# Half of the output projection's contraction as three fp32r products, with the first expert weights split ahead of the expert stage

## The reference

```python
qkv = modulate(x) @ w_in                          # 640 x 1024 @ 1024 x 3072
na_o = neighbourhood_or_dense_attention(...)      # 8 heads x 64
df_o = rms_norm(softmax(q1 k1) v - lam * softmax(q2 k2) v) * (1 - lambda_init)   # 4 heads x 128
o = concat([na_o, df_o])                          # 640 x 1024
x1 = layer_norm(ALPHA * x + gate1 * (o @ w_out))  # w_out 1024 x 1024
aff = softmax(modulate(x1) @ w_router)            # 16 experts
g, idx = top_k(aff.T, cap)                        # 64 latent + 16 context tokens for each expert
y = (silu(xs @ w_gate) * (xs @ w_up)) @ w_down * g       # d_ff 2816, fp32 weights, 553 MB in all
out = layer_norm(ALPHA * x1 + gate2 * scatter_add(y))
```

## Time and profile before

| | us |
|---|---|
| median of 3 runs (lowest, highest) | 2013.46 (2012.74, 2016.18) |
| the profiled execution | 2015.8 |
| its span, first to last instruction | 2014.0 |
| PE busy | 1940.7 (96%) |
| DVE busy | 1651.3 (82%) |
| ACT busy | 1378.8 (68%) |
| POOL busy | 182.9 (9%) |

### The profile page before, as it was taken

The page is one execution under the profiler, slowest core; times in us unless marked ns, Lnnn a source line. Parts: engine busy times, 40 slices in busy tenths (PEclk is TensorE's granted clock), DMA queues, the critical chain, the costliest instruction groups (busy, mean ns, idle before and its releaser), DMA issues.

```text
span 2014.0 us, 25015 instructions
## 1 busy us (share of the span) xinstructions
PE 1940.7 (96%) x9564; PEld 1327.3 (66%) x9564; DVE 1651.3 (82%) x1627; ACT 1378.8 (68%) x1618; POOL 182.9 (9%) x98
## 2 busy tenths in 40 slices
PE   8999889984999999999999999999999999999998
PEld 8999666652666666666666666666666666666664
DVE  3766556677989889898989898988989898989896
ACT  3222255644787877778787878787777878787875
POOL 0000212121010101010101101010101010110100
PEclk9999789995999999999999999999999999999999
DMA  9544601133999999999999999999999999999994
GB/s 380 198 155 170 218 27 54 58 117 125 405 343 407 362 413 359 388 376 372 385 369 394 360 398 348 404 355 401 360 384 376 374 387 368 393 360 395 353 388 158
DMA packets 100998, 636.32 MB, mean 316 GB/s; under 512 B 11569, under 2 KB 19761, under 8 KB 28049
## 3 DMA queue, kind: packets, MB, share of 16 engines
q1 hardware_dynamic: 96048, 618.23, 78.5%
q0 software_dynamic: 4832, 16.50, 3.2%
HBM read 620.02 MB, written 13.88 MB: 315 GB/s over the span
## 4 chain that ended last, share of the span: by engine, by line
PE 75%; ACT 1%; DVE 1%; issue 0%; DVEq 0%; ACTq 0%
PE ps L1430 16%; PE ps L1429 16%; PE ps L1434 16%; PE ps L1446 8%; PE ps L1447 8%; PE ps L1451 8%; PE ps L1409 1%; PE ps L1400 0%; DVE place L1608 0%; ACT place L1533 0%; DVE place L1550 0%; PE ps L1469 0%; ACT place L1497 0%; ACT place L1536 0%; ACT L1536 0%; ACT place L1531 0%
## 5 line engine op out<-in xcount | busy, mean ns | idle before, releaser
L1550 DVE TENSOR_TENSOR place<-ring,place 128x2048 fp32r<-128x2048 f32 x528 | 1226.6, 2335 | 150.8 <-ACT place L1497 147.4
L1497 ACT ACTIVATE place<-ring 128x2048 fp32r<-128x2048 f32 x528 | 1010.1, 1916 | 334.1 <-PE ps L1434 234.3
L1429 PE MATMUL ps<-place 128*80 128x512 f32 x1408 | 561.0, 398 | 4.9 <-DVE place L1544 4.9
L1430 PE MATMUL ps<-place 128*80 128x512 f32 x1408 | 555.5, 395 | 0.0
L1434 PE MATMUL ps<-place 128*80 128x512 f32 x1408 | 381.4, 392 | 0.0
L1434 PEld LDWEIGHTS ps<-place 128*80 128x80 f32 x1408 | 208.2, 148 | 115.8 <-issue 0.7
L1429 PEld LDWEIGHTS ps<-place 128*80 128x80 f32 x1408 | 208.5, 148 | 110.5 <-DVE place L1544 5.1
L1446 PE MATMUL ps<-place 128*80 128x512 f32 x704 | 280.5, 398 | 0.0
L1430 PEld LDWEIGHTS ps<-place 128*80 128x80 f32 x1408 | 209.2, 149 | 107.2 <-issue 0.7
L1447 PE MATMUL ps<-place 128*80 128x512 f32 x704 | 277.1, 394 | 0.0
L1451 PE MATMUL ps<-place 128*80 128x512 f32 x704 | 190.4, 392 | 0.0
(11 more groups left out here) (189 smaller groups left out, 1708.4 us busy)
## 6 DMA issues: line engine op xcount, KB each, us to landing
ring<-in_w_exp SPq DMA_DIRECT2D x528, 1024.0 KB, 7.1
ring<-in_w_late SPq DMA_DIRECT2D x16, 1024.0 KB, 11.0
ring<-in_w_in SPq DMA_DIRECT2D x12, 1024.0 KB, 6.9
ring<-in_w_ada SPq DMA_DIRECT2D x8, 1024.0 KB, 10.2
ring<-in_w_out SPq DMA_DIRECT2D x4, 1024.0 KB, 6.3
place<-in_near_bias SPq DMA_DIRECT2D x16, 256.0 KB, 3.2
ring<-in_xT SPq DMA_DIRECT2D x4, 640.0 KB, 9.1
place<-in_x SPq DMA_DIRECT2D x5, 512.0 KB, 6.5
```

The source lines that it names most:

```text
L1429: eng.matmul(out, xH[:, e % 2, kk, :], w, start=(kk == 0), stop=False)
L1430: eng.matmul(out, xL[:, e % 2, kk, :], w, start=False, stop=False)
L1497: eng.activation(wH[:, n % SPLITS, :], ring[:, slot("exp", n), :], ACT.Copy).then_inc(wh_done, 1)
L1550: eng.tensor_tensor(wL[:, n % SPLITS, :], ring[:, slot("exp", n), :], wH[:, n % SPLITS, :].bitcast(F32), ALU.subtract).then_inc(chunk_used, 1)
```

## The change

1. **Output projection.** For contraction tiles 0 to 3 of each half the product is three fp32r products. ACT rounds `out` chunks 0 and 2 into two free ring slots in steps 1 and 2 (`round_out`), POOL writes the remainders over the raw chunks (two tensor_tensor of 128 x 2048). ACT copies the first half of the turned tile into `OTH` (rounded); DVE takes the remainder `OTL` from PSUM (`split_turned`, first thing in the step after "turn o"). Tiles 4 to 7 stay fp32. PE waits for the new semaphores `out_split` and `ot_split`.
2. **Ring.** The two free slots are those that the first two expert chunks had. All four `out` chunks are issued in the first block, no expert chunk is; the six first expert chunks are issued when the last tile's projection has let their slots go, three after half 0 and three after half 1.
3. **First expert chunks.** `high(0)`, `high(1)` run at the end of ACT's attention block, `low(0)`, `low(1)` on POOL, after its last `start_sum` and ahead of the gather.
4. **Projection block.** The rotary products come after `values(i, 0)`, the context keys' transposes after `values(i, 2)`.
5. **Memory.** Tiles are packed anew (`mod_c` in `scr`, `tie` and `rowA` in `far`, `Xg` and others moved).

```diff
-                for n in range(n, FIRST + 2):
+                for n in range(n, FIRST):
                     issue(eng, n)
...
-                for n in range(FIRST + 2, FIRST + RING):
+                eng.wait_ge(out_used, 2)
+                for n in (FIRST + 3, FIRST + 2, FIRST):
+                    issue(eng, n)
+                eng.wait_ge(out_used, 4)
+                for n in (FIRST + 5, FIRST + 4, FIRST + 1):
                     issue(eng, n)
...
+        def out_high(half):
+            return ring_rounded[:, (FIRST + half) % RING, :]
+        def out_low(half):
+            return ring_rounded[:, slot("out", 2 * half), :]
...
                 for k in range(STEPS):
+                    if k in (1, 2):
+                        eng.wait_ge(out_rounded, k)
+                        eng.tensor_tensor(out_low(k - 1), ring[:, slot("out", 2 * (k - 1)), :], out_high(k - 1).bitcast(F32),
+                                          ALU.subtract).then_inc(out_split, 1)
...
                     start_sum(s)
+                for n in range(READY):
+                    low(eng, n)
...
+                        if j < HALF_K:
+                            eng.matmul(ps[:, bank, :], OTH[:, j, :], wh, start=(j == 0), stop=False)
+                            eng.matmul(ps[:, bank, :], OTL[:, j, :], wh, start=False, stop=False)
+                            mm = eng.matmul(ps[:, bank, :], OTH[:, j, :], wl, start=False, stop=(j == final))
...
+                def round_out(half):
+                    arrived(eng, "out", 2 * half)
+                    eng.wait_ge(*released(FIRST + half - RING))
+                    eng.activation(out_high(half), ring[:, slot("out", 2 * half), :], ACT.Copy).then_inc(out_rounded, 1)
...
+                def split_turned(s, part, tiles):
+                    use = turn_no["o", s, part]
+                    eng.wait_ge(t_copied, use + 1)
+                    c0 = P * (part == 2)
+                    n = P * len(tiles)
+                    out, high = (x[:, tiles[0]:tiles[-1] + 1, :].rearrange("p k t -> p (k t)") for x in (OTL, OTH))
+                    eng.tensor_tensor(out, ps[:, 4 + use % 2, c0:c0 + n], high.bitcast(F32), ALU.subtract).then_inc(ot_split, 1)
...
                 for k in range(STEPS):
+                    if due("turn o", k - 1) is not None:
+                        split_turned(due("turn o", k - 1), 0, range(HALF_K))
                     if 1 <= k:
                         combine(k - 1)
```

More of the change, by code:

```diff
@@ L82, in sem @@
             return ctx.enter_context(nc.semaphore(name))
+        with nc.sbuf_tensor("ring_rounded", [P, RING, CW], F32R) as ring_rounded:
+            pass
         ring = ctx.enter_context(nc.sbuf_tensor("ring", [P, RING, CW], F32))
@@ L119, in build @@
         places.append(ctx.enter_context(ExitStack()))
-        qna, qdf = (b.rearrange("p (i t) -> p i t", i=GROUPS) for b in (shared, take(GROUPS * TOK)))
-        Xg = shared[:, 0:2 * D].rearrange("p (b d) -> p b d", b=2)
-        X32 = shared[:, 2 * D:2 * D + HALF_K * CAP].rearrange("p (k s) -> p k s", k=HALF_K)
+        qna, qdf = (take(GROUPS * TOK).rearrange("p (i t) -> p i t", i=GROUPS) for _ in range(2))
         kna, kdf = (take(GROUPS * (TOK + CTX)).rearrange("p (i t) -> p i t", i=GROUPS) for _ in range(2))
@@ L323, in _ @@
                         project(i, g)
-                    for t in range(3):
-                        values(i, t)
+                    values(i, 0)
                     if i == 0:
@@ L338, in _ @@
                     mm.then_inc(kctx_ready, 1)
+                    values(i, 3)
                     values(i, 4)
@@ L402, in _ @@
                         high(3 * i + 3)
-                    for t in range(4):
+                    for t in range(3):
                         copy_values(i, t)
@@ L635, in build, with splits_by, high, low @@
             turn_no[use] = len(turn_no)
+        def splits_by(n):
+            return sum(1 for use, m in turn_no.items() if m <= n and use[0] == "o" and use[2] in (0, 2))
         def turned(s):
-            return OT if s < END else Pb[:, UNITS % 2, 0:D].rearrange("p (k t) -> p k t", k=KT)
+            return OT if s < END else Pb[:, UNITS % 2, 0:D // 2].rearrange("p (k t) -> p k t", k=HALF_K)
+        def out_high(half):
+            return ring_rounded[:, (FIRST + half) % RING, :]
+        def out_low(half):
+            return ring_rounded[:, slot("out", 2 * half), :]
         def heads_of(s, part):
             return range(GROUPS) if s < END else (range(3), range(3, GROUPS))[part]
+        def high(eng, n):
+            arrived(eng, "exp", n)
+            eng.activation(wH[:, n % SPLITS, :], ring[:, slot("exp", n), :], ACT.Copy).then_inc(wh_done, 1)
+        def low(eng, n):
+            eng.wait_ge(wh_done, n + 1)
+            eng.tensor_tensor(wL[:, n % SPLITS, :], ring[:, slot("exp", n), :], wH[:, n % SPLITS, :].bitcast(F32),
+                              ALU.subtract).then_inc(chunk_used, 1)
         def fetch(eng, e):
@@ L1028, in _ @@
                     eng.wait_ge(t_ready, use + 1)
-                    eng.activation(turned(END)[:, HALF_K * part:HALF_K * part + 3, :].rearrange("p k t -> p (k t)"),
+                    eng.activation((turned(END) if part else OTH)[:, 0:3, :].rearrange("p k t -> p (k t)"),
                                    ps[:, 4 + use % 2, 0:3 * P], ACT.Copy).then_inc(t_copied, 1)
@@ L1040, in _ @@
                 raise_logits(END)
+                for n in range(READY):
+                    high(eng, n)
             @block.vector
@@ L1245, in _ @@
                 share(END - 2)
+                split_turned(END, 0, range(3))
                 gated(END - 1, 1)
@@ L1250, in _ @@
                 keep_shares(END - 2)
+                split_turned(END, 2, range(3, 4))
                 first_half(range(0, 2))
```

135 lines of the change are left out of this document (74 added, 61 removed).

## The result

The changed kernel is slower. Its median over 20 runs is 2016.8 us (2013.32 to 2022.8), that of the kernel before over 20 runs on the same chip 2012.03 (2008.88 to 2016.18): ratio 1.0028, 95% interval 1.0020 to 1.0035, or 5.6 us by the ratio. I had forecast 3.65 us less. The profiled execution took 2019.35 us with a span of 2017.5.

A forecast was written before the change was run, and what follows sets the result against it. PE was taken to bound the expert stage and, nearly, attention from step 7 to the last tile, with chains around it. Terms -2.1 - 4.8 - 0.65 + 1.0 + 0.2 + 6.0 - 3.3 = -3.65 gave 2009.8 us, range 2003.3 to 2016.

The forecast's parts named there:

- Weights rounded and split in steps 1 and 2: Early attention: POOL's two weight subtractions hold DVE's two-input operations, 6.0 us lost, bounds 0 and 9.8.
- The fp32r products: Output projection on PE: 0.68 us gained per group, seven groups counting, 4.8 us gained.
- the remainder of the turned tile: DVE's extra subtraction before PE's next projection, tiles 1 to 3: 1.0 us lost in all.
- the clock stays low: Rival, 13%: longer standstill in steps 3 and 4 brings more low clock; 2014.8, or 2019.8 in its long form.
- The last remainders on POOL: Before the gather: POOL's first expert-weight remainders end at 472.3, ahead of the merge at 473.78; nothing lost.
- The expert stage's start: First expert chunks rounded and split ahead, so the first expert product starts at 485.45, not 488.75: 3.3 us gained.
- The block's end: End of projection block: context keys' store issued earlier, next block starts 2.1 us sooner, bounds 0 and 2.5.
- The last tile's 0.65: Last tile's output projection: PE's saving, less DVE's two more subtractions, leaves 0.65 us gained.
- ACT's roundings: Steps 1 and 2: two weight roundings fit nearly whole into ACT's waits, 0.2 us lost, at most 3.8.
- POOL writes rounded values: Rival, 7%: POOL writes rounded values more slowly, delaying the attention's end; 2027.9 at twice the 4.9 us.
- DVE isn't held: Rival, 17%: POOL's weight subtractions let DVE in, so the 6.0 us loss falls away; 2003.8.
- The scaling holds DVE too: Rival, 8%: POOL's one-input scalings behind the subtractions also hold DVE, some 2.5 us more; 2012.3.

The follow-up runs named there:

- run 12: Changed kernel with each of POOL's two 128 x 2048 weight subtractions cut into four slices of 512 columns; one execution, no median given.
- run 2: Changed kernel with output-projection weights rounded by ACT and their remainders taken by DVE at the projection block's end, not by POOL in the attention; 2008.83 us, ratio 0.998.
- run 9: Changed kernel, weights split in first block, last three expert loads behind last rows' store, POOL's sums for tiles 1 and 2 behind head scaling; 2003.53 us, ratio 0.9949.
- run 1: Changed kernel with the whole output projection back in plain fp32, the rest of the change kept; 2007.74 us, ratio 0.9979.
- run 10: Changed kernel, output projection in fp32, last three expert loads behind last rows' store, POOL's sums for tiles 1 and 2 behind head scaling; 2004.69 us, ratio 0.9956.
- run 5: Changed kernel with weights split in the first block and POOL's sums for tiles 0 to 2 waiting for DVE's head scaling; 2009.01 us.
- run 4: Changed kernel with the last three expert loads issued behind the last rows' store, their order turned round; 2014.98 us, ratio 1.0013.
- run 7: Changed kernel, weights split in first block, POOL's sums for tiles 0 to 2 behind head scaling, last three expert loads behind last rows' store; 2005.78 us.
- run 8: Changed kernel, output projection in fp32, POOL's sums for tiles 0 to 2 behind head scaling, last three expert loads behind last rows' store; 2005.96 us.
- run 11: Kernel before with only the new order of values, rotary and transposing products in the projection block; 2009.82 us, ratio 0.9987.
- run 13: Changed kernel with POOL's two 128 x 2048 weight subtractions replaced by one-input multiplications by zero of the same size; one execution, no median given.
- run 6: Changed kernel with the output projection in fp32 and POOL's sums for tiles 0 to 2 waiting for DVE's head scaling; 2006.79 us.
- run 3: Changed kernel with the first two remainders of expert weights taken by DVE instead of POOL; 2016.75 us, ratio 1.0025.

## Why the prediction was wrong

It said 2009.8 (2003.3 to 2016.0), a small gain. What was measured is 5.6 us slower, 9.3 off. (Its chances for the single cases add to 106%, a slip; the three for faster, same and slower are as they stand.)

Up to the first expert product the forecast's terms make -3.65 us and the shifts +4.16. Of these 7.8 us, 7.1 lie between the scores of step 17 and the norm of tile 3, 2.7 at the merge and 2.4 in step 3; larger gains than foreseen elsewhere, some of them lent by the low clock in the profile of the kernel before, hide 4.3.

**The first step that failed** is "Weights rounded and split in steps 1 and 2", the +6.0. The mechanism was the right one and POOL's length too (4.48 each for 4.9). What failed is that I let `combine` in between the two operations: "held until 242.5", and then only the next step's products in the second. POOL's subtractions follow each other without a gap, and DVE is held through all of them (run 12) and 1.2 us of the scaling. The loss is 8.56 us in the profile and 8.0 by the medians (run 2). My bound of 9.8 was both operations in full; I gave it no weight.

**The fp32r products** (-4.8): a group gains 0.55, not 0.68, which makes 3.9 for seven. The five up to step 15 gave about 1.9 of 2.75 (runs 2 and 9 against 1 and 10). The difference is what I had booked under the remainder of the turned tile: PE reaches the products of half 0 later in its step by 0.13, 0.41 and 0.20 us in steps 11, 15 and 19, 0.7 in all for 1.0. The last two groups, in steps 17 and 19, came to nothing here and in run 2: PE is earlier at a tile that DVE isn't done with, and what follows costs more than a group gives (6.4 us lost in run 2 from step 17 to the norm of tile 3, 1.2 in step 17 of run 9). In run 9, with the holds gone, run 10 falls behind by 1.0 us between step 18 and the norm of tile 3. I had taken PE's 187 busy us of 200 as closed from step 7 on, though the earlier trace rows leave 13.

**The largest miss** is the loss in steps 17 and 20, for which I had no term: 6.04 us. The earlier trace rows showed the hold in step 20, and I wrote that this row "doesn't move with PE". It does: POOL's sum starts when the rows' store has landed, DVE's scaling where PE's order puts it. DVE lost 0.5 us against POOL in step 20 and was 0.9 us earlier against it in step 17, and that turned three scalings of 2.97 into 5.03, and the first square of step 17 from 0.37 into 1.26 (1.60 in run 2). With POOL's sums put behind them both rows were short again and the loss was gone (run 5). PE's waits of 1.78 and 2.24 were followed by 0.50 of the clock. My rival "the clock stays low" had the price, but the place wrong: steps 3 and 4, where the chain is.

**The last remainders on POOL** (0, "with 1.5 us to spare"): 2.68 lost. The duration was right (4.48 for 4.9); the start wasn't. I had dismissed the six loads as in time for ACT and never asked what they do to POOL's store: POOL waited 7.82 us for it, not 3.72. With the loads behind the store the merge isn't held (runs 4 and 7 to 10).

**What held.** The expert stage's start: 3.11 for 3.3. The block's end came earlier as foreseen, but by 3.06 for 2.1 and beyond my bound of 2.5: I took 1.26 us from the last copy to the new block where it was 0.28, and part of it is the ring's (run 11: 1.37 for the order alone). The last tile's 0.65 is open: from the norm of tile 3 to that of tile 4 run 2 gains 1.3 over run 1, but run 9 gains nothing over run 10 (16.41 and 16.44 us). ACT's roundings (1.92 and 1.91) lie in its waits as foreseen, and POOL writes rounded values at no extra cost (4.48 us for 2048 columns, 2.35 for 1024 in fp32), so that rival is out. The rival "DVE isn't held" is refuted by the row of 9.08 us and by run 12. "The scaling holds DVE too" was partly right: in the changed kernel the small product at 246.12 lasts 1.28, until 1.08 us after the second scaling's start, but no longer; the row at 241.27 of the kernel before, which I had overlooked, says the same. The Trainium skill (SBUF — State Buffer, section Who interferes with whom) makes no exception for a POOL operation with one input; run 13 agrees that such an operation holds DVE, and shows that it doesn't do so for its whole length.

**Still open:** why the one-input operation lets DVE in before its end, and whether the fp32r products are worth anything in this kernel. In the four pairs that differ by them and their remainders, fp32r is 1.1 and 2.2 us slower by the medians (runs 2 and 1, 5 and 6) and 0.2 and 1.2 faster (7 and 8, 9 and 10). What made runs 9 and 10 fast is the rest of the change and the waits on POOL and SP.

## What to carry to other kernels

When work goes to an idle engine, list every operation of another engine that its work can hold, and take a run of operations without a gap as one hold, however it is sliced. Before crediting PE with faster products, look at what it next waits for, and price a longer wait with the clock that follows it. A hold seen once is a matter of timing between two engines; ask what it becomes when one of them comes 2 us earlier, and try a wait on the quiet engine (with it and the rest of the change, runs 9 and 10 were 8.3 and 9.5 us under the kernel before).

## What the runs showed of the hardware

- A DVE operation with two inputs in SBUF stayed held through eight two-input POOL operations without a gap (9.80 us, run 12) and through two (9.08 in the changed kernel; 2.93 in run 5). Between two that lay 0.08 us apart it was let in (step 20 of the changed kernel).
- In the merge a DVE operation with one input was held too (2.86 us for 0.18), and in run 3 a DVE subtraction held POOL's issue of the gather (2.59 us for 0.98).
- A POOL operation with one input (128 x 2048, 5.38 us) held DVE for its first 3.7 to 3.8 us; one of 128 x 1024 (2.78) for 1.1 to 1.2.
- A subtraction of 128 x 2048 takes 4.48 us on POOL and 2.29 on DVE.
- fp32r products with 128 stationary columns and 512 moving start 0.233 us apart at full clock and 0.43 at 0.50; an fp32 one takes 0.86.
- From step 15 to the norm of tile 3 PE had eleven waits of 1.54 to 2.47 us in the changed kernel and runs 2, 4, 5, 7, 12 and 13, and at or behind every one the granted clock fell to 0.50 (1.2 GHz) for 3.4 or 6.8 us. Behind waits of 1.10 to 1.15 us it fell in run 9 and did not in runs 1, 5 and 7; behind one of 0.81 us (step 13 of run 7) it fell.
- POOL waited 7.8 us behind the issue of a 512 KB store beside SP's loads, 3.2 without them (run 4). The 128 KB store at the first block's end landed in 4.6 and 6.2 us beside expert chunks, in 2.3 without.
- In three of thirteen profiled experiments (runs 5, 6, 8) the clock was 0.83 from 20 to 40 us, and everything behind came about 3 us later, also in kernels that are alike up to there.
